# The sixth operand's low half behind the last first-layer norm, POOL's weight differences in two pieces, and one sum in halves

## The chip, the cores and the metric

The kernel runs on one core of a Trainium2 chip. The core has a matrix engine (PE, with its weight loads as PEld), a vector engine (DVE), a scalar engine (ACT), a third elementwise engine (POOL) and SyncE (SP), which issues the transfers. They run separate instruction streams and wait for one another by semaphores. The metric is device time in microseconds (us) for one execution, lower is better.

## The reference, cut to what matters

One decoder layer on 1024 tokens of width 1024, in float32. Two attentions run side by side, their outputs are gated, merged and projected, a layer norm follows, and then the MLP:

```python
merged = gate_a * (ya @ w_branch_a) + gate_b * (yb @ w_branch_b)
mix_out = merged @ w_out
x = _layer_norm(DEEPNORM_ALPHA * x + mix_out, ln1_gain, ln1_bias)   # the first-layer norm
h = square(relu(x @ w_ff1))                                        # 1024 -> 4096
ff_out = h @ w_ff2                                                 # 4096 -> 1024
x = _layer_norm(DEEPNORM_ALPHA * x + ff_out, ln2_gain, ln2_bias)
```

## The kernel before, in words

A float32 product is made of three matmuls. An operand is split into a high half (a copy rounded to the matrix engine's float32 format, made by ACT) and a low half (operand minus high half, made by DVE or POOL by one subtraction); the three matmuls are high by high, low by high and high by low.

The MLP's products use Strassen's scheme in Winograd's form: seven block products in place of eight, on sums and differences of the four blocks of each operand. In the first MLP product the seven are numbered m = 1 to 7. `x_h`, `x_l` hold the high and low halves of the activation operand of each m, `a_h`, `a_l` those of the weight operand; the work runs in eight rounds n = 0 to 7 over the 4096 hidden columns. A product (n, m) is 24 matmuls of 512 columns in two halves t = 0, 1 of 12, one PSUM bank each (`up`, L1094 to L1114). Round 0 takes m in the order 1, 2, 6, 5, 7, 4, 3 (`UP_FIRST`); the sums of the products (`take_u2`, `take_u3`, `take_c22`, ...) run on DVE. Product 7 adds to the banks of product 6, and `take_u3` adds to them `p1`, the first product, into `c22`; product 4 then adds to the same banks again, so PE may start it only when `take_u3` has read them.

The change lies where the output projection ends and round 0 begins. Tokens come in eight blocks `tb` of 128. For each, PE makes `project_out(tb)` in two halves of 24 matmuls, DVE adds the residual and norms the row block (`layer_norm1`, L1921), PE transposes the result (`turn_x1`, L1049, 8 transposes), and ACT and DVE split it (`x_high`, `x_low`) and form the sums. The last block's transposes stand inside product (0, 2), behind its ninth matmul. There is no planner: each engine's order is written by hand, and an engine that waits holds up all that stands behind it in its own order.

- DVE, after the norm of block 6 (`layer_norm1(TB - 2, 0, 64)`): `sums_low(6, 0, 3)`, the low half of the sixth activation operand for its first three column blocks (1536 columns, one subtraction with both inputs in SBUF); then the norm of block 7, between whose two halves `x_low(TB - 2)` makes low halves 1 and 2 that product (0, 1) and (0, 2) wait for; then `x_low(TB - 1)`, which reads the last transposes.
- POOL: `a_low(1)`, `a_low(2)` (low halves of weight operands, L2360), `r_s1 = r21 + r22` (L2369), `r11 = r_s1 - r11` (L2372), `a_low(6)`: five instructions of 1024 columns.
- ACT: `a_high(5, 0)`, which waits for `r_s1`, `a_high(6, 0)`, which waits for the second sum (`w_sum`), and behind it `x_high(TB - 1)`, the high halves of the last transposed block (L1414 to L1418).
- PE: product (0, 1) waits for the first low half out of `x_low(TB - 2)` (`x1_lo` 7) and for `a_lo[1]`; the transposes of block 7 wait for `x1_ready`, the end of the norm (L1918); product (0, 6) waits for `a_lo[6]` and for the sixth operand's last block (`x_low_done` 2).

In rows of the profile, L1587 is the helper that subtracts (`sub`), L1988 that of `add`, L1991 that of `minus`. Names there lack buffer numbers and last digits: `r` stands for `r11`, `r12`, `r21` and `r22`, `r_s` for `r_s1`, `b_f` for `b11_f` and `b21_f`, `t_last` for `t2_last`, `c` for `c22` and its like.

Of the kernel before, what the change touches and what calls it, by code (L numbers as in the profile page):

```python
# [18 lines left out]
F32 = mybir.dt.float32  # L19
# [70 lines left out]
for _n in range(ITERS):  # L90
    for _m in UP if _n else UP_FIRST:
        UP_END[_m, _n] = len(UP_END) + 2
# [96 lines left out]
def layer_kernel(nc, x, w_in, w_branch_a, w_branch_b, w_out, lambda_q1, lambda_k1, lambda_q2,  # L189
                 lambda_k2, subln_gain, ln1_gain, ln1_bias, w_ff1, w_ff2, ln2_gain, ln2_bias,  # L190
                 consts, rope, out):
    with ExitStack() as ctx:
# [207 lines left out]
        x22_f = sem("x22_f")  # L400
# [5 lines left out]
        up_done, p1_read, c11_read, taken = sem("up_done"), sem("p1_read"), sem("c11_read"), sem("taken")  # L406
        relu_done, h_sum = sem("relu_done"), sem("h_sum")
# [342 lines left out]
        def _(pe):  # L750
# [310 lines left out]
            def wait_up(n, m):  # L1061
# [27 lines left out]
                elif m == 4:  # L1089
                    pe.wait_ge(taken, 5 * n + 2)  # L1090
                elif m == 3:
                    pe.wait_ge(taken, 5 * n + 3)

            def up(n, m):  # L1094

                wait_up(n, m)
                for t in range(2):
                    if n == 0 and m == 2:
                        pe.wait_ge(p1_read, t + 1)
                    o = up_bank(m, t)  # L1100
# [11 lines left out]
                    if n == 0 and m == 1 and t == 0:  # L1112
# [59 lines left out]
        def _(act):  # L1172
# [229 lines left out]
            def x_high(tb):  # L1402
# [9 lines left out]
                else:  # L1412
                    act.wait_ge(t12_ready, 2 * j + 2)
                    act.activation(x_block(6, 0, j), x_sum(6, j), ACT.Copy).then_inc(t_hi, 1)  # L1414
                    act.activation(x_sum(3, j), by_block(p_proj[:, 1, :]), ACT.Copy).then_inc(x22_f, 1)
# [167 lines left out]
        def _(dve):  # L1583
# [304 lines left out]
            def layer_norm(row, tb, s, base_n, summed, scale_here, stat=None, gain=None):  # L1888
# [3 lines left out]
                for h in range(2):  # L1892
# [28 lines left out]
            def layer_norm1(tb, s, count, between=lambda: None):  # L1921
                for h in range(2):
                    if h == 1:
                        between()
# [6 lines left out]
                layer_norm(rows[s][:, :], tb, s, 0, lambda h: dve.wait_ge(o_read, tb * 2 + (h + 1)), True)\  # L1931
# [44 lines left out]
            layer_norm1(TB - 2, 0, 64)  # L1976
            sums_low(6, 0, 3)
            layer_norm1(TB - 1, 1, 64, lambda: x_low(TB - 2))
# [43 lines left out]
            def take_u3(n):  # L2022
                dve.wait_ge(up_done, UP_END[7, n])
                if n:
                    dve.wait_ge(s_h[4], 16 * n)
                    dve.wait_ge(h_sum, 4 * n - 3)
                else:
                    dve.wait_ge(s_x1[1], 64)
                    dve.wait_ge(x1_turned, 2 * TB)
                add(c22, bank_b, p1).then_inc(taken, 1)  # L2030

            def take_c22(n):
                dve.wait_ge(up_done, UP_END[5, n])
                dve.wait_ge(taken, 5 * n + 2)
                add(c22, bank_c, c22).then_inc(taken, 1)
# [215 lines left out]
        def _(pool):  # L2251
# [105 lines left out]

            def a_low(m):
                pool.wait_ge(a_hi, HIGH_END[m, 0])
                pool.tensor_tensor(al[m][:, :, :], raw[m][:, :, :], ah[m][:, :, :].bitcast(F32), ALU.subtract)\  # L2360
                    .then_inc(a_lo[m], 1)
# [39 lines left out]
```

## Time and profile before

| | |
|---|---|
| Time of three executions | 1502.28, 1504.42, 1505.61 us; median 1504.42 |
| Execution that was profiled | 1502.67 us, its span 1500.6 us |
| PE busy in the span | 1469.0 us, 98% |
| DVE, ACT, POOL busy | 990.9 us (66%), 664.2 us (44%), 353.6 us (24%) |
| Mean granted clock of PE | 0.997 of full speed |
| PE idle between 855 and 925 us | three times: 0.63, 0.77 and 1.41 us |

The span runs from the first to the last instruction; the execution's time has 2.07 us more. A matmul of 512 columns is shown with 0.39 us, but in an unbroken row the next one starts 0.227 us later, so the shown durations overlap. Idle time in brackets is that before the row, with what ended it.

### The profile page before, as it was taken

Reading aid. Unit: us, or ns where it says so; the run is one execution under the profiler, and the core shown is the slowest. Engines: PE = TensorE matmul, PEld = TensorE weight load, DVE = VectorE, ACT = ScalarE, POOL = GpSimd, SP = SyncE. Lnnn points to the kernel's source line nnn. Section 1 sums busy time; section 2 is a strip of 40 time slices with the busy share of each in tenths; the row PEclk is TensorE's granted clock in tenths of the full one; section 3 lists DMA queues with packets and bytes.
Section 4 is the critical chain, followed back from the end, with each engine's and each line's share of the span. In section 5 each row is a group of like instructions: output and inputs, shape, how many; then the busy total and the mean of one; then the engine's idle time right before and its main releaser. Section 6 shows DMA issues by size and latency. Waiting matters only on the chain.

```text
span 1500.6 us, 19376 instructions
## 1 busy us (share of the span) xinstructions
PE 1469.0 (98%) x7152; PEld 1220.7 (81%) x7152; DVE 990.9 (66%) x1232; ACT 664.2 (44%) x1035; POOL 353.6 (24%) x276
## 2 busy tenths in 40 slices
PE   8999999999999999999999999999999999999997
PEld 6788888887888887888778877888888888888886
DVE  3676776768857557444466688766664477668767
ACT  3455554556556556442022244444443434433343
POOL 2635445355444244210230040000000000000004
PEclk9999999999999999999999999999999999999999
DMA  5101112111111101011343224444442678835563
GB/s 179 57 28 57 57 43 71 56 56 54 46 57 28 29 15 42 28 57 43 126 154 127 85 98 155 182 163 149 152 154 99 237 277 277 316 123 191 193 200 135
DMA packets 111504, 172.41 MB, mean 115 GB/s; under 512 B 6080, under 2 KB 71616, under 8 KB 111296
## 3 DMA queue, kind: packets, MB, share of 16 engines
q1 hardware_dynamic: 111424, 171.33, 33.5%
q8 instruction: 51, 0.84, 0.2%
q14 instruction: 29, 0.24, 0.1%
HBM read 127.27 MB, written 44.04 MB: 114 GB/s over the span
## 4 chain that ended last, share of the span: by engine, by line
PE 87%; DVE 6%; issue 3%; DMA 2%; ACT 1%; POOL 1%; SPq 0%; DVEq 0%; ACTq 0%
PE p_proj L760 8%; PE p_proj L756 8%; PE p_proj L758 8%; PE p_z L1108 5%; PE p_z L1106 5%; PE p_z L1110 5%; PE p_z L1128 4%; PE p_z L1129 4%; PE p_z L1130 4%; PE p_tr L858 3%; PE p_z L795 2%; PE p_av L872 2%; PE p_z L791 2%; PE p_av L875 2%; PE p_proj L1108 2%
## 5 line engine op out<-in xcount | busy, mean ns | idle before, releaser
L756 PE MATMUL p_proj<-xt_h,w_hi 128*128 128x512 f32 x640 | 253.9, 397 | 0.6 <-DVE xt_l L1587 0.6
L760 PE MATMUL p_proj<-xt_h,w_lo 128*128 128x512 f32 x640 | 252.7, 395 | 0.0
L758 PE MATMUL p_proj<-xt_l,w_hi 128*128 128x512 f32 x640 | 251.2, 393 | 0.0
L2262 POOL TENSOR_TENSOR w_lo<-w_raw,w_hi 128x512 fp32r<-128x512 f32 x96 | 133.7, 1414 | 223.1 <-DVE w_hi L1594 222.6
L2378 POOL TENSOR_TENSOR row_odd<-row_odd,gains 128x1024 f32<-128x1024 f32 x4 | 10.4, 2621 | 580.1 <-ACT row_odd L1559 580.1
L760 PEld LDWEIGHTS p_proj<-xt_h,w_lo 128*128 128x128 f32 x640 | 120.3, 188 | 23.6
L756 PEld LDWEIGHTS p_proj<-xt_h,w_hi 128*128 128x128 f32 x640 | 120.4, 188 | 22.8 <-DVE xt_l L1587 0.6
L758 PEld LDWEIGHTS p_proj<-xt_l,w_hi 128*128 128x128 f32 x640 | 120.5, 188 | 20.8
L1587 DVE TENSOR_TENSOR d_al<-f_a,d_ah 128x1024 fp32r<-128x1024 f32 x56 | 68.5, 1224 | 78.8 <-ACT d_ah L1477 78.8
L1477 ACT ACTIVATE d_ah<-f_a 128x1024 fp32r<-128x1024 f32 x56 | 59.2, 1057 | 133.2 <-PE p_av L1130 54.9
L1330 ACT ACTIVATE a_t<-p_tr 128x384 fp32r<-128x384 f32 (+3 forms) x96 | 47.2, 492 | 123.6 <-PE p_tr L858 123.5
L1106 PE MATMUL p_z<-x_h,a_h 128*128 128x512 f32 x256 | 99.8, 390 | 0.6 <-DVE x_l L1587 0.6
L1110 PE MATMUL p_z<-x_h,a_l 128*128 128x512 f32 x256 | 99.6, 389 | 0.0
L1108 PE MATMUL p_z<-x_l,a_h 128*128 128x512 f32 x256 | 99.6, 389 | 0.0
L1128 PE MATMUL p_z<-d_bh,d_ah 128*128 128x512 f32 x256 | 99.6, 389 | 0.0
L1129 PE MATMUL p_z<-d_bl,d_ah 128*128 128x512 f32 x256 | 99.6, 389 | 0.0
L1130 PE MATMUL p_z<-d_bh,d_al 128*128 128x512 f32 x256 | 99.6, 389 | 0.0
L1437 ACT ACTIVATE a_h<-r 128x1024 fp32r<-128x1024 f32 x48 | 50.4, 1056 | 88.1 <-PE p_z L1110 47.6
L1587 DVE TENSOR_TENSOR a_t<-p_tr,a_t 128x384 fp32r<-128x384 f32 (+3 forms) x96 | 53.0, 552 | 52.1 <-ACT a_t L1330 51.8
L1594 DVE CAST w_hi<-w_raw 128x1024 fp32r<-128x1024 f32 x48 | 43.4, 905 | 59.5 <-DMA w_raw<-w_branch_b 34.2
L1587 DVE TENSOR_TENSOR a_l<-r,a_h 128x1024 fp32r<-128x1024 f32 x45 | 54.9, 1219 | 37.0 <-ACT a_h L1437 37.0
L1699 DVE TENSOR_REDUCE vecs<-p_z 128x1 f32<-128x128 f32 (+7 forms) x64 | 46.9, 753 | 42.0 <-PE p_z L795 41.7
(287 smaller groups left out, 3546.7 us busy)
## 6 DMA issues: line engine op xcount, KB each, us to landing
f_a<-h_terms SPq DMA_DIRECT2D x56, 512.0 KB, 3.4
w_raw<-w_in SPq DMA_DIRECT2D x40, 512.0 KB, 3.9
h_terms<-c SPq DMA_DIRECT2D x40, 512.0 KB, 3.1
f_b<-w_ff SPq DMA_DIRECT2D x40, 512.0 KB, 4.7
r<-w_ff SPq DMA_DIRECT2D x32, 512.0 KB, 4.0
gate_rows<-gst SPq DMA_DIRECT2D x12, 512.0 KB, 5.0
y<-x SPq DMA_DIRECT2D x8, 512.0 KB, 8.6
wo_raw<-w_out SPq DMA_DIRECT2D x8, 512.0 KB, 8.8
```

The source lines that it names most:

```text
L756: pe.matmul(o, w_hi[n_slot][:, k, :], xt_h[:, k, cols], start=(k == 0), stop=False)
L758: pe.matmul(o, w_hi[n_slot][:, k, :], xt_l[:, k, cols], start=False, stop=False)
L760: mm = pe.matmul(o, w_lo[n_slot][:, k, :], xt_h[:, k, cols], start=False, stop=(k == KT - 1))
L1106: pe.matmul(o, ah[m][:, k, cols], x_row(m, 0, k), start=fresh and k == 0, stop=False, skip_group_check=not fresh)
L1108: pe.matmul(o, ah[m][:, k, cols], x_row(m, 1, k), start=False, stop=False, skip_group_check=not fresh)
L1110: mm = pe.matmul(o, al[m][:, k, cols], x_row(m, 0, k), start=False, stop=k == 3, skip_group_check=not fresh)
L1128: pe.matmul(o, a_h[:, t, rws], b_h[:, t, :], start=first, stop=False, skip_group_check=more)
L1129: pe.matmul(o, a_h[:, t, rws], b_l[:, t, :], start=False, stop=False, skip_group_check=more)
L1130: return pe.matmul(o, a_l[:, t, rws], b_h[:, t, :], start=False, stop=last, skip_group_check=more)
L1477: act.activation(a_h[:, :, :], f_a[g % 2][:, :, :], ACT.Copy).then_inc(d_hi, 1)
L1587: return dve.tensor_tensor(o, a, b.bitcast(F32), ALU.subtract)
L2262: low = pool.tensor_tensor(w_lo[slot][:, ks, :], w_raw[:, ks, :], w_hi[slot][:, ks, :].bitcast(F32), ALU.subtract)
```

## The change

Four edits.

1. `sums_low(6, 0, 3)` moves on DVE from ahead of the last `layer_norm1` to behind it. In that last norm the statistics of the first half are taken ahead of `x_low(TB - 2)`, not together with those of the second half.
2. On POOL each of the five instructions becomes two of 512 columns; the semaphore is raised by the second.
3. In round 0, `take_u3` becomes two instructions, one for each half of product 7. The first raises the new semaphore `u3_half`, and the first half of product (0, 4) waits for that alone; the second half waits for `taken`. To that end product (0, 7) counts its first half in `up_done`, and the table `UP_END` shifts by one.
4. The semaphore `x22_f`, for which nothing waited, is dropped.

On DVE, around the last first-layer norm. `x_l_112` is the sixth operand's low half, `x_l_111` and `x_l_116` are those of the first and second; `rows_105` is block 7. Before:

```order
L1918 SCALAR_TENSOR_TENSOR rows_104<-rows_104,vecs,gains 128x1024 [waits dve_own]
L1587 TENSOR_TENSOR x_l_112<-x_f_120,x_h_108 128x4x384 [waits t34_ready,t_hi]
L1929 SCALAR_TENSOR_TENSOR rows_105<-rows_105,p_z 128x512 [waits row_in1,o_done]
L1587 TENSOR_TENSOR x_l_111<-p_proj,x_h_107 128x4x128 [waits x1_hi]
L1587 TENSOR_TENSOR x_l_116<-p_proj,x_h_115 128x4x128 [waits x1_hi]
L1929 SCALAR_TENSOR_TENSOR rows_105<-rows_105,p_z 128x512 [waits o_done]
L1895 BN_STATS vecs<-rows_105 128x6 [waits o_read] x2
```

The same place in the change:

```order
L1923 SCALAR_TENSOR_TENSOR rows_104<-rows_104,vecs,gains 128x1024 [waits dve_own]
L1940 SCALAR_TENSOR_TENSOR rows_105<-rows_105,p_z 128x512 [waits row_in1,o_done]
L1934 BN_STATS vecs<-rows_105 128x6 [waits o_read]
L1592 TENSOR_TENSOR x_l_111<-p_proj,x_h_107 128x4x128 [waits x1_hi]
L1592 TENSOR_TENSOR x_l_116<-p_proj,x_h_115 128x4x128 [waits x1_hi]
L1940 SCALAR_TENSOR_TENSOR rows_105<-rows_105,p_z 128x512 [waits o_done]
L1900 BN_STATS vecs<-rows_105 128x6 [waits o_read]
```

The long subtraction is gone from here, and the first half's statistics stand ahead of the two low halves that PE waits for. It comes back behind the last pass of that norm, ahead of the last transposes' first sum:

```order
L1914 TENSOR_SCALAR vecs<-vecs 128x1 [waits dve_own]
L1917 TENSOR_SCALAR vecs<-vecs 128x1 [waits dve_own]
L1923 SCALAR_TENSOR_TENSOR rows_105<-rows_105,vecs,gains 128x1024 [waits dve_own]
L1592 TENSOR_TENSOR x_l_112<-x_f_120,x_h_108 128x4x384 [waits t34_ready,t_hi]
L1956 TENSOR_TENSOR x_f_121<-p_proj,b_f 128x4x128 [waits xe_f,x1_turned]
```

What was ahead of the norm now follows it.

POOL in the same stretch, before (`a_l_130`, `a_l_131`, `a_l_132` are the low halves of weight operands 1, 2 and 6; `r_137` is `r11`):

```order
L2360 TENSOR_TENSOR a_l_130<-r_137,a_h_123 128x1024 [waits a_hi]
L2360 TENSOR_TENSOR a_l_131<-r_138,a_h_124 128x1024 [waits a_hi]
L2369 TENSOR_TENSOR r_s_141<-r_139,r_140 128x1024 [waits r22_in,r21_in]
L2372 TENSOR_TENSOR r_137<-r_s_141,r_137 128x1024 [waits a_lo1,w_sum]
L2360 TENSOR_TENSOR a_l_132<-r_137,a_h_125 128x1024 [waits a_hi]
```

And in the change:

```order
L2379 TENSOR_TENSOR a_l_130<-r_137,a_h_123 128x512 [waits a_hi]
L2379 TENSOR_TENSOR a_l_130<-r_137,a_h_123 128x512
L2379 TENSOR_TENSOR a_l_131<-r_138,a_h_124 128x512 [waits a_hi]
L2379 TENSOR_TENSOR a_l_131<-r_138,a_h_124 128x512
L2390 TENSOR_TENSOR r_s_141<-r_139,r_140 128x512 [waits r22_in,r21_in]
L2390 TENSOR_TENSOR r_s_141<-r_139,r_140 128x512
L2395 TENSOR_TENSOR r_137<-r_s_141,r_137 128x512 [waits a_lo1,w_sum]
L2395 TENSOR_TENSOR r_137<-r_s_141,r_137 128x512
L2379 TENSOR_TENSOR a_l_132<-r_137,a_h_125 128x512 [waits a_hi]
L2379 TENSOR_TENSOR a_l_132<-r_137,a_h_125 128x512
```

The order is the same, in two pieces each, and the second pieces have no wait.

DVE at the third sum of round 0 in the change (`c_147` is `c22`; before, its first two rows were one of 128x1024 at L1988, and L2038, L2040 are the halves):

```order
L2002 TENSOR_TENSOR r_138<-r_138,r_137 128x1024 [waits a_lo2,w_sum]
L2038 TENSOR_TENSOR c_147<-p_z,p_142 128x512 [waits up_done,x1_turned,s_x1_1]
L2040 TENSOR_TENSOR c_147<-p_z,p_142 128x512 [waits up_done]
L1999 TENSOR_TENSOR c_147<-p_proj,c_147 128x1024 [waits u3_half,taken,up_done]
L1592 TENSOR_TENSOR a_l_136<-r_138,a_h_129 128x1024 [waits a_hi]
L1592 TENSOR_TENSOR res_r<-res,res_r 128x16x128 [waits x1_hi,t_hi]
```

Only the split is new there; what follows keeps its order.

The diff:

```diff
--- before.py
+++ after.py
@@ -89,7 +89,7 @@
 UP_END, HIGH_END = {}, {}
 for _n in range(ITERS):
     for _m in UP if _n else UP_FIRST:
-        UP_END[_m, _n] = len(UP_END) + 2
+        UP_END[_m, _n] = len(UP_END) + (3 if _n or _m in UP_FIRST[4:] else 2)
 for _m in (1, 2, 5, 6, 7, 4, 3):
     HIGH_END[_m, 0] = len(HIGH_END) + 1
 for _n in range(ITERS):
@@ -397,13 +397,13 @@
         s_x1 = [sem("s_x1_0"), sem("s_x1_1")]
         x1_turned = sem("x1_turned")
         xe_f, x1_hi, x1_lo = sem("xe_f"), sem("x1_hi"), sem("x1_lo")
-        x22_f = sem("x22_f")
         t12_ready, t34_ready, t_hi = sem("t12_ready"), sem("t34_ready"), sem("t_hi")
         x_low_done = sem("x_low_done")
         r11_in, r12_in, r21_in, r22_in = sem("r11_in"), sem("r12_in"), sem("r21_in"), sem("r22_in")
         w_sum, a_hi = sem("w_sum"), sem("a_hi")
         a_lo = {m: sem(f"a_lo{m}") for m in UP}
         up_done, p1_read, c11_read, taken = sem("up_done"), sem("p1_read"), sem("c11_read"), sem("taken")
+        u3_half = sem("u3_half")
         relu_done, h_sum = sem("relu_done"), sem("h_sum")
         sq_done = {m: sem(f"sq_done{m}") for m in (11, 21, 12, 22)}
         s_h = {m: sem(f"s_h{m}") for m in UP}
@@ -1087,7 +1087,10 @@
                 elif m == 2 and n > 0:
                     pe.wait_ge(p1_read, n + 2)
                 elif m == 4:
-                    pe.wait_ge(taken, 5 * n + 2)
+                    if n:
+                        pe.wait_ge(taken, 5 * n + 2)
+                    else:
+                        pe.wait_ge(u3_half, 1)
                 elif m == 3:
                     pe.wait_ge(taken, 5 * n + 3)
 
@@ -1097,6 +1100,8 @@
                 for t in range(2):
                     if n == 0 and m == 2:
                         pe.wait_ge(p1_read, t + 1)
+                    if n == 0 and m == 4 and t == 1:
+                        pe.wait_ge(taken, 2)
                     o = up_bank(m, t)
                     cols = slice(t * P, (t + 1) * P)
                     fresh = m in (1, 6, 5)
@@ -1109,7 +1114,7 @@
                                   skip_group_check=not fresh)
                         mm = pe.matmul(o, al[m][:, k, cols], x_row(m, 0, k), start=False, stop=k == 3,
                                        skip_group_check=not fresh)
-                    if n == 0 and m == 1 and t == 0:
+                    if n == 0 and m in (1, 7) and t == 0:
                         mm.then_inc(up_done, 1)
                 mm.then_inc(up_done, 1)
 
@@ -1412,7 +1417,7 @@
                 else:
                     act.wait_ge(t12_ready, 2 * j + 2)
                     act.activation(x_block(6, 0, j), x_sum(6, j), ACT.Copy).then_inc(t_hi, 1)
-                    act.activation(x_sum(3, j), by_block(p_proj[:, 1, :]), ACT.Copy).then_inc(x22_f, 1)
+                    act.activation(x_sum(3, j), by_block(p_proj[:, 1, :]), ACT.Copy)
                     act.activation(x_block(3, 0, j), by_block(p_proj[:, 1, :]), ACT.Copy).then_inc(x1_hi, 1)
                     act.wait_ge(t12_ready, 2 * j + 1)
                     act.activation(x_block(5, 0, j), x_sum(5, j), ACT.Copy).then_inc(t_hi, 1)
@@ -1885,11 +1890,11 @@
             sub(m_l[0][:, last_k, :], res[:, last_k, 0:P], m_h[0][:, last_k, :]).then_inc(mt_lo, 1)
             merged_low(1, 1)
 
-            def layer_norm(row, tb, s, base_n, summed, scale_here, stat=None, gain=None):
+            def layer_norm(row, tb, s, base_n, summed, scale_here, stat=None, gain=None, halves_due=(0, 1)):
 
 
                 st = stats[s] if stat is None else stat
-                for h in range(2):
+                for h in halves_due:
                     if summed is not None:
                         summed(h)
                         own(dve.bn_stats(st[:, 6 * h:6 * h + 6], row[:, h * NH:(h + 1) * NH]))
@@ -1918,9 +1923,15 @@
                 return dve.scalar_tensor_tensor(out=row, in0=row, scalar=ln_r[s],
                                                 in1=gains[:, 1, :], op0=ALU.mult, op1=ALU.add)
 
-            def layer_norm1(tb, s, count, between=lambda: None):
+            def layer_norm1(tb, s, count, between=lambda: None, stats_early=False):
+                def summed(h):
+                    dve.wait_ge(o_read, tb * 2 + (h + 1))
+
                 for h in range(2):
                     if h == 1:
+                        if stats_early:
+                            summed(0)
+                            own(dve.bn_stats(stats[s][:, 0:6], rows[s][:, 0:NH]))
                         between()
                     dve.wait_ge(o_done, tb * 2 + (h + 1))
                     if h == 0:
@@ -1928,7 +1939,7 @@
                     cols = slice(h * NH, h * NH + NH)
                     dve.scalar_tensor_tensor(out=rows[s][:, cols], in0=rows[s][:, cols], scalar=ALPHA,
                                              in1=p_z[s][:, cols], op0=ALU.mult, op1=ALU.add).then_inc(o_read, 1)
-                layer_norm(rows[s][:, :], tb, s, 0, lambda h: dve.wait_ge(o_read, tb * 2 + (h + 1)), True)\
+                layer_norm(rows[s][:, :], tb, s, 0, summed, True, halves_due=(1,) if stats_early else (0, 1))\
                     .then_inc(x1_ready, 1)
 
             def x_low(tb):
@@ -1974,8 +1985,8 @@
                 merged_low(tb + 2, tb % 2)
                 x_low(tb)
             layer_norm1(TB - 2, 0, 64)
+            layer_norm1(TB - 1, 1, 64, lambda: x_low(TB - 2), True)
             sums_low(6, 0, 3)
-            layer_norm1(TB - 1, 1, 64, lambda: x_low(TB - 2))
             x_low(TB - 1)
 
 
@@ -2020,18 +2031,23 @@
                 add(u2, bank_b, p1).then_inc(taken, 1)
 
             def take_u3(n):
-                dve.wait_ge(up_done, UP_END[7, n])
-                if n:
-                    dve.wait_ge(s_h[4], 16 * n)
-                    dve.wait_ge(h_sum, 4 * n - 3)
-                else:
+                if n == 0:
                     dve.wait_ge(s_x1[1], 64)
                     dve.wait_ge(x1_turned, 2 * TB)
+                    dve.wait_ge(up_done, UP_END[7, 0] - 1)
+                    dve.tensor_tensor(c22[:, 0, :], up_bank(7, 0), p1[:, 0, :], ALU.add).then_inc(u3_half, 1)
+                    dve.wait_ge(up_done, UP_END[7, 0])
+                    dve.tensor_tensor(c22[:, 1, :], up_bank(7, 1), p1[:, 1, :], ALU.add).then_inc(taken, 1)
+                    return
+                dve.wait_ge(up_done, UP_END[7, n])
+                dve.wait_ge(s_h[4], 16 * n)
+                dve.wait_ge(h_sum, 4 * n - 3)
                 add(c22, bank_b, p1).then_inc(taken, 1)
 
             def take_c22(n):
                 dve.wait_ge(up_done, UP_END[5, n])
                 dve.wait_ge(taken, 5 * n + 2)
+                dve.wait_ge(u3_half, 1)
                 add(c22, bank_c, c22).then_inc(taken, 1)
 
             def take_c21(n):
@@ -2355,10 +2371,14 @@
                 pool.tensor_tensor(x_sum(7, j), x_sum(6, j), b11_f[:, :, :], ALU.subtract).then_inc(t34_ready, 1)
                 pool.tensor_tensor(x_sum(4, j), b21_f[:, :, :], x_sum(6, j), ALU.subtract).then_inc(t34_ready, 1)
 
+            pieces = (slice(0, 2), slice(2, 4))
+
             def a_low(m):
                 pool.wait_ge(a_hi, HIGH_END[m, 0])
-                pool.tensor_tensor(al[m][:, :, :], raw[m][:, :, :], ah[m][:, :, :].bitcast(F32), ALU.subtract)\
-                    .then_inc(a_lo[m], 1)
+                for ks in pieces:
+                    low = pool.tensor_tensor(al[m][:, ks, :], raw[m][:, ks, :], ah[m][:, ks, :].bitcast(F32),
+                                             ALU.subtract)
+                low.then_inc(a_lo[m], 1)
 
             for j in range(3):
                 sums(j)
@@ -2366,10 +2386,14 @@
             a_low(2)
             pool.wait_ge(r21_in, 16)
             pool.wait_ge(r22_in, 16)
-            pool.tensor_tensor(r_s1[:, :, :], r21[:, :, :], r22[:, :, :], ALU.add).then_inc(w_sum, 1)
+            for ks in pieces:
+                sums_of = pool.tensor_tensor(r_s1[:, ks, :], r21[:, ks, :], r22[:, ks, :], ALU.add)
+            sums_of.then_inc(w_sum, 1)
             pool.wait_ge(w_sum, 1)
             pool.wait_ge(a_lo[1], 1)
-            pool.tensor_tensor(r11[:, :, :], r_s1[:, :, :], r11[:, :, :], ALU.subtract).then_inc(w_sum, 1)
+            for ks in pieces:
+                sums_of = pool.tensor_tensor(r11[:, ks, :], r_s1[:, ks, :], r11[:, ks, :], ALU.subtract)
+            sums_of.then_inc(w_sum, 1)
             a_low(6)
 
             for q in range(TB - 1):
```

## Rows read from the trace of the kernel before

**Rows 1.** Timeline of PE: start us, us, engine, line, operation, shapes, count [idle before <-releaser].

```profile
878.59 0.39 PE L1031 MATMUL p_z<-wo_h,m_l 128*128 128x512 f32 x1
879.61 0.47 PE L1106 MATMUL p_z<-x_h,a_h 128*128 128x512 f32 x1 [0.63 <-DVE x_l L1587]
...
888.15 1.09 PE L1049 MATMUL p_proj<-small,rows 128*128 128x128 f32 x8 [0.77 <-DVE rows L1918]
...
892.51 0.39 PE L1106 MATMUL p_z<-x_h,a_h 128*128 128x512 f32 x1
...
908.61 0.39 PE L1110 MATMUL p_z<-x_h,a_l 128*128 128x512 f32 x1
910.41 0.47 PE L1106 MATMUL p_z<-res_r,a_h 128*128 128x512 f32 x1 [1.41 <-DVE c L1988]
...
915.93 0.39 PE L1106 MATMUL p_proj<-res_r,a_h 128*128 128x512 f32 x1
```

**Rows 2.** Timeline of DVE, 874 to 892 us.

```profile
874.33 3.94 DVE L1587 TENSOR_TENSOR x_l<-x_f,x_h 128x1536 fp32r<-128x1536 f32 x1
...
879.98 0.67 DVE L1929 SCALAR_TENSOR_TENSOR rows<-rows,p_z 128x512 f32<-128x512 f32 x1
...
882.20 2.55 DVE L1901 SCALAR_TENSOR_TENSOR rows<-rows,vecs,gains 128x1024 f32<-128x1024 f32 x1
...
885.61 2.48 DVE L1918 SCALAR_TENSOR_TENSOR rows<-rows,vecs,gains 128x1024 f32<-128x1024 f32 x1
...
891.03 0.69 DVE L1587 TENSOR_TENSOR x_l<-t_last,x_h 128x512 fp32r<-128x512 f32 x1 [0.70 <-ACT x_h L1414]
```

**Rows 3.** Timeline of POOL, 873 to 891 us.

```profile
873.38 3.27 POOL L2360 TENSOR_TENSOR a_l<-r,a_h 128x1024 fp32r<-128x1024 f32 x1 [2.50 <-ACT a_h L1437]
878.93 2.39 POOL L2360 TENSOR_TENSOR a_l<-r,a_h 128x1024 fp32r<-128x1024 f32 x1 [2.28 <-ACT a_h L1437]
881.27 2.40 POOL L2369 TENSOR_TENSOR r_s<-r,r 128x1024 f32<-128x1024 f32 x1
883.75 3.26 POOL L2372 TENSOR_TENSOR r<-r_s,r 128x1024 f32<-128x1024 f32 x1
888.24 2.40 POOL L2360 TENSOR_TENSOR a_l<-r,a_h 128x1024 fp32r<-128x1024 f32 x1 [1.23 <-ACT a_h L1437]
```

**Rows 4.** Timeline of POOL and DVE, earlier: POOL work already in two pieces.

```profile
561.31 2.98 POOL L2262 TENSOR_TENSOR w_lo<-w_raw,w_hi 128x512 fp32r<-128x512 f32 x2 [0.63 <-DVE w_hi L1594]
...
617.88 2.55 POOL L2262 TENSOR_TENSOR w_lo<-w_raw,w_hi 128x512 fp32r<-128x512 f32 x2 [13.19 <-DVE w_hi L1594]
...
562.38 0.76 DVE L1669 TENSOR_TENSOR stage<-stage,swap 128x512 f32<-128x512 f32 x1
```

**Rows 5.** Timeline of ACT, 876 to 891 us.

```profile
876.34 0.59 ACT L1411 ACTIVATE x_h<-p_proj 128x512 fp32r<-128x512 f32 x1
...
887.11 1.06 ACT L1437 ACTIVATE a_h<-r 128x1024 fp32r<-128x1024 f32 x1 [0.19 <-POOL r L2372]
890.36 0.63 ACT L1414 ACTIVATE x_h<-t_last 128x512 fp32r<-128x512 f32 x1 [2.20 <-DVE t_last L1949]
```

**Rows 6.** Timeline of DVE around the third sum of round 0.

```profile
909.03 1.23 DVE L1988 TENSOR_TENSOR c<-p_z,p 128x1024 f32<-128x1024 f32 x1 [1.85 <-PE p_z L1110]
910.36 1.23 DVE L1988 TENSOR_TENSOR c<-p_proj,c 128x1024 f32<-128x1024 f32 x1
...
912.64 2.29 DVE L1587 TENSOR_TENSOR res_r<-res,res_r 128x2048 fp32r<-128x2048 f32 x1
```

**Rows 7.** Stretches: from:to, length, busy of PE, PEld, DVE, ACT, POOL, granted clock, DMA.

```profile
671.00:675.00 4.00, 4.00 (x11) 3.13 (x10) 0.00 (x0) 2.62 (x3) 0.00 (x0) 0.50 0.01 2
782.50:785.30 2.80, 0.00 (x0) 0.03 (x1) 2.80 (x3) 0.00 (x0) 0.48 (x1) 1.00 0.00 0
...
1492.50:1493.00 0.50, 0.28 (x2) 0.00 (x0) 0.18 (x1) 0.00 (x0) 0.49 (x1) 1.00 0.00 0
...
1497.50:1498.00 0.50, 0.00 (x0) 0.00 (x0) 0.50 (x1) 0.00 (x0) 0.00 (x0) 0.75 0.02 8
```

## The prediction

> **What bounds the kernel now.** I read the shares of the page first: PE is busy for 98% of the span, so only its few gaps can be won or lost. The timeline of PE over the stretch that the change touches shows three of them, which a DVE instruction ends each time: 0.63 us ahead of product (0, 1), 0.77 ahead of the last transposes, 1.41 ahead of product (0, 4) [rows 1]. In an unbroken row a matmul starts 0.227 us after the last and is shown with 0.39, so a gap costs its idle time plus 0.16: 879.61 - 878.59 - 0.23 = 0.79, then 0.93, then 910.41 - 908.61 - 0.23 = 1.57 [rows 1]. A product of 24 matmuls takes 5.44 us, but 5.52 behind a gap (910.41 to 915.93) [rows 1]: 0.08 to 0.12 more for each. All that the change can win is thus 3.29 + 0.3 = some 3.6 us, 0.24% of the time; 0.2%, 3.0 us, is about what a measurement of this kernel can tell from no change.
>
> Then I read DVE and POOL side by side, and that is the view that decides here. The 1536-column subtraction takes 3.94 us, and 2048 columns take 2.29 elsewhere [rows 2, 6]. POOL was at work until 873.38 + 3.27 = 876.65, and DVE ends 1.62 us after that. The norm's two passes show the same: POOL ends at 883.67 and DVE's pass at 884.75, 1.08 later; POOL at 887.01, DVE at 888.09, 1.08 later [rows 2, 3]. And the other way round: POOL's second sum starts at 883.75 behind that DVE pass and takes 3.26 in place of 2.40 [rows 3]. So a DVE instruction that reads two tensors from SBUF and a POOL instruction shut each other out, and the later one waits for the end of the earlier. With one input from PSUM DVE is free of it (879.98: 0.67 us while POOL is at work) [rows 2, 3].
>
> **The change part by part.** I run the clock of before on from 874.33, where DVE's order first differs.
>
> *The move.* Without the subtraction DVE does the first half row at 874.33 and its statistics, and is idle when ACT ends the first high half at 876.34 + 0.59 = 876.93 [rows 5]. The low half that PE waits for is there at 877.6, not 879.5; PE comes at 878.59 + 0.23 = 878.82 and goes on. Gap 1 is gone: 0.79 + 0.12. DVE takes the second half row 0.42 us after PE's last matmul's start (the lag of 908.61 to 909.03) [rows 1, 6], at 879.01 in place of 879.98. From there to the norm's first pass it took 2.22 us [rows 2]; one set of statistics less (0.60) makes 1.62, so that pass is ready at 880.63.
>
> *The pieces.* Two pieces take 2.55 us where one instruction takes 2.39 [rows 3, 4], so 0.15 more for each of the five. What happens between the pieces is seen in the earlier stretch: two pieces from 561.31 take 2.98, and a DVE pass issued at 562.38 ends at 563.14, that is 0.56 us after the first piece (561.31 + 1.27); the second ends 1.15 after DVE [rows 4]. DVE slips in between and POOL pays. With these numbers, in turn: POOL's second low half 878.93 to 881.47; DVE's first pass to 882.55; POOL piece to 883.70; DVE's second pass, ready at 883.4 (its small steps take 885.61 - 884.75 = 0.86 [rows 2]), to 884.78. The row block is normed at 884.8 in place of 888.09. PE reaches the transposes at 878.82 + 33 x 0.227 = 886.3: gap 2 is gone too, 0.93 + 0.1.
>
> The Trainium skill ("SBUF — State Buffer", section "Who interferes with whom") says of this port pair that issue order, not the shape of the operation, decides who blocks. By it the DVE pass that was issued first goes ahead of POOL's second piece; [rows 4] agree, with 0.56 us behind the first piece. Were it otherwise, rival B below would hold.
>
> *What the move now lands on.* Behind the norm stands the 1536-column subtraction. It is ready at 884.8, in the middle of POOL's sums, where before it had delayed only DVE. POOL's piece goes to 885.93, the subtraction to 887.55 (1.62), POOL's second sum to 888.70 and, unhindered, 889.97 (before: 887.01). Three DVE instructions, 1.08 + 1.08 + 1.62 = 3.78 us, now lie inside POOL's chain of second low half and two sums, where one pass of 1.08 lay before. For this sum ACT waits with the high half of weight operand 6: 890.07 to 891.13 (before 887.11) [rows 5], and POOL's low half of it starts at 891.20, not 888.24 [rows 3]. ACT's next, the high half of the last block, starts at 891.0 in place of 890.36 and gives DVE its low half (two SBUF inputs) at 891.7; that slips between POOL's pieces: 892.46, DVE to 893.01, POOL to 894.16. Before, POOL was done at 890.64 and PE came at 892.51, so 1.9 us of cover lay there [rows 1, 3]. Now PE comes at 886.3 + (892.51 - 888.15) = 890.67 and may go on about 0.15 us after 894.16 (DVE's 909.03 + 1.23 let PE go at 910.41 [rows 1, 6]), at 894.3. A new gap: 3.6 us, as idle time 3.5, in front of product (0, 6), which starts 1.8 us later than before. For the bounds of this unknown: with neither the subtraction nor the low half in POOL's way (2.17 us less) it starts at 892.1; with one more DVE pass in the way (1.1 to 2.2) at 895.4 to 896.5.
>
> *The third sum.* Product (0, 4)'s first half needs only the first half of the sum, which DVE can make while PE does product 7's second half (DVE was idle for 1.85 us there [rows 6]). Gap 3 goes: 1.57 + 0.08. Product (0, 4) starts at 894.3 + 5.52 + 2 x 5.44 = 910.70 (before 910.41). DVE is 0.54 us sooner with its sums, since 0.69 stands where 1.23 was; but the low half for product (0, 3) ended at 912.64 + 2.29 = 914.93 and PE came at 915.93 [rows 1, 6], with 1.0 us of cover less lag. In the new clock it is there at 916.25 and lets PE go at 916.40, while PE comes at 916.14: a small gap, 0.26 + 0.08.
>
> *Sum.* Won: 0.91 + 1.03 + 1.65 = 3.6. Lost: 3.6 + 0.1 + 0.34 = 4.05. Product (0, 3) ends 0.5 us later than before. From there to the end PE has no gap in either, so the shift goes through. The dropped semaphore, the extra one in `take_c22` and 8 instructions more on POOL and DVE, off PE's path, cost nothing: `u3_half` is raised before the sum that asks for it. The profiled execution took 1502.67 us and becomes 1503.2; the median of the runs shown is 1.75 above it, so the forecast is 1504.9.
>
> **The rivals.** *A. The port's delays fall elsewhere and the new gap stays away*: 3.6 - 0.34 = 3.25 us won, 1501.2. For it: a DVE pass in POOL's way costs nothing where POOL has time, as before at 1.9 us of cover. Against it: POOL's chain would have to be 3.6 us shorter than I find, nearly all of the 4.3 us of DVE work that I put into it, and PE comes 1.85 us sooner.
>
> *B. POOL keeps the port through both pieces.* Then DVE's first pass waits for the end of POOL's first sum (884.0, to 885.1), the second for that of the second sum (887.5, to 888.6); the transposes start 0.55 later than before, product (0, 6) too, and gap 3 less 0.34 is won: 0.55 - 1.65 + 0.34 = -0.75, 1503.7. Against it: DVE's pass between two pieces at 562.38 [rows 4].
>
> *C. The new gap lets PE's clock fall*, and the kernel is slower. The longest gap in the middle of the program is 2.8 us and the clock stayed at 1.00; after the last matmul (ended 1492.78) it was still 1.00 at first and 0.75 in the half microsecond from 1497.5, so it fell within 4.7 to 5.2 us [rows 7]. My gap of 3.5 lies between. If it falls, matmuls run as at 671 to 675, at 0.50, the lower level of 1.2 GHz: 11 in 4 us [rows 7] where 4 / 0.227 = 17.6 fit, so 4 us of it lose 1.5, and 6 us at half the pace lose 3. The time is then 0.5 + 1.5 to 3 above: 1506.4 to 1507.9, about 1507.2. It decides between 2.8 and 4.7 us of idle time in front of product (0, 6); a gap of 4.5, if one more DVE pass comes in between, brings it near.
>
> **How the numbers follow.** Forecast 75%, A 6%, B 7%, C 12%. The forecast's own range is what the bounds give: product (0, 6) 2.2 sooner to 2.2 later, of which I hold the ends unlikely, so -1.5 to +2 with the spread of the runs (1502.28 to 1505.61) around the median: 1502.4 to 1506.9. C lies at the upper edge, A below the lower: I take 1502.0 to 1507.2. Slower by over 0.2% (above 1507.4) is half of C and a bad tail, 9%; faster by over 0.2% (under 1501.4) is A and a little, 7%; within 84%.
>
> **What would show it.** In the profile after: no gap in front of product (0, 1) nor of the last transposes; POOL's pieces of the two sums with three waits of 1.1 to 1.6 us among them, ending near 890; ACT's high half of operand 6 starting about 3 us later than 887.11; a gap of 3 to 4 us in front of product (0, 6), ended by POOL's low half; none in front of product (0, 4), one of some 0.1 to 0.3 in front of (0, 3). The forecast is wrong if POOL's last low half ends under 891, if DVE's passes wait through both pieces, or if the granted clock is under 1.00 after that gap.

## The result, and the profile after

The changed kernel takes 1507.74 us in the median of 21 executions, the one before 1504.65 us in 21 of its own: a ratio of 1.0020, 95% interval 1.0013 to 1.0028, so 2.0 to 4.2 us slower. The forecast was 0.5 us slower and the range ended at 1507.2. The profiled execution took 1506.52 us, span 1504.7.

The timeline of PE in the changed kernel, where before had its three gaps (columns as in [rows 1]; L1111 is the old L1106, L2379 the old L2360, L1999 the old L1988); the last row is from round 1:

```profile
891.92 0.39 PE L1115 MATMUL p_z<-x_h,a_l 128*128 128x512 f32 x1
895.71 0.80 PE L1111 MATMUL p_z<-x_h,a_h 128*128 128x512 f32 x1 [3.40 <-POOL a_l L2379]
896.30 0.63 PE L1113 MATMUL p_z<-x_l,a_h 128*128 128x512 f32 x1
896.73 0.63 PE L1115 MATMUL p_z<-x_h,a_l 128*128 128x512 f32 x1
...
902.85 0.39 PE L1111 MATMUL p_proj<-x_h,a_h 128*128 128x512 f32 x1
...
918.95 0.39 PE L1115 MATMUL p_z<-res_r,a_l 128*128 128x512 f32 x1
919.37 0.47 PE L1111 MATMUL p_proj<-res_r,a_h 128*128 128x512 f32 x1
...
952.68 0.47 PE L1111 MATMUL p_z<-res_r,a_h 128*128 128x512 f32 x1 [0.38 <-DVE c L1999]
```

All three gaps of [rows 1] are gone. In their place stand one of 3.40 us in front of product (0, 6), ended by POOL's low half, one of 0.19 in front of product (0, 3) (919.37 - 918.95 - 0.23; the rows show no idle time for it), and one of 0.38 in round 1. And behind the first of them matmuls are shown with 0.63 us and start 0.43 apart, not 0.23: product (0, 6) takes 902.85 - 895.71 = 7.14 us where 5.52 was its time. The stretches show why (columns as in [rows 7]):

```profile
785.00:786.00 1.00, 0.78 (x4) 0.67 (x5) 1.00 (x2) 0.00 (x0) 0.00 (x0) 1.00 0.00 0
...
787.00:788.00 1.00, 1.00 (x4) 0.81 (x3) 0.62 (x2) 0.45 (x2) 0.00 (x0) 0.50 0.00 0
...
894.00:895.00 1.00, 0.00 (x0) 0.00 (x0) 1.00 (x2) 0.65 (x2) 1.00 (x1) 1.00 0.00 0
895.00:896.00 1.00, 0.29 (x1) 0.29 (x2) 1.00 (x1) 0.00 (x0) 0.66 (x1) 0.85 0.00 0
896.00:897.00 1.00, 1.00 (x3) 0.81 (x3) 1.00 (x3) 0.76 (x2) 0.00 (x0) 0.50 0.00 0
897.00:898.00 1.00, 1.00 (x3) 0.72 (x3) 1.00 (x1) 0.47 (x1) 0.00 (x0) 0.50 0.00 0
```

The granted clock fell to 0.50 (1.2 GHz) at the end of the new gap, and 8 matmuls ran at it: 8 x 0.2 = 1.6 us. It also fell near 786 us, 1.2 us after the end of the 2.82 us gap that both kernels have. In the profile of before it had stayed at 1.00 in that gap [rows 7] and behind it:

```profile
785.30:790.00 4.70, 4.70 (x21) 3.88 (x22) 3.63 (x4) 1.26 (x2) 0.00 (x0) 1.00 0.27 77
```

Timelines of DVE, POOL and ACT in the changed kernel, for the chain that ends the new gap:

```profile
875.85 0.68 DVE L1940 SCALAR_TENSOR_TENSOR rows<-rows,p_z 128x512 f32<-128x512 f32 x1
...
882.32 1.76 DVE L1906 SCALAR_TENSOR_TENSOR rows<-rows,vecs,gains 128x1024 f32<-128x1024 f32 x1
...
884.93 1.38 DVE L1923 SCALAR_TENSOR_TENSOR rows<-rows,vecs,gains 128x1024 f32<-128x1024 f32 x1
886.24 2.84 DVE L1592 TENSOR_TENSOR x_l<-x_f,x_h 128x1536 fp32r<-128x1536 f32 x1
```

```profile
880.46 2.54 POOL L2379 TENSOR_TENSOR a_l<-r,a_h 128x512 fp32r<-128x512 f32 x2 [2.13 <-ACT a_h L1442]
882.95 4.52 POOL L2390 TENSOR_TENSOR r_s<-r,r 128x512 f32<-128x512 f32 x2
887.54 3.95 POOL L2395 TENSOR_TENSOR r<-r_s,r 128x512 f32<-128x512 f32 x2
892.72 2.94 POOL L2379 TENSOR_TENSOR a_l<-r,a_h 128x512 fp32r<-128x512 f32 x2 [1.23 <-ACT a_h L1442]
```

```profile
891.58 1.06 ACT L1442 ACTIVATE a_h<-r 128x1024 fp32r<-128x1024 f32 x1 [2.96 <-POOL r L2395]
```

DVE reaches its first changed instruction at 875.85 here, not 874.33: this execution is 1.52 us later before the change begins. The fall near 786 us accounts for that: PE had started its output projection 0.08 us sooner (785.22 for 785.30) and then had 8 slow matmuls. Less 1.52, DVE's two passes end at 882.56 and 884.79, the moved subtraction at 887.56, POOL's second sum at 889.97, ACT starts at 890.06, and POOL ends at 894.14. The forecast had 882.55, 884.78, 887.55, 889.97, 890.07, 894.16.

### The profile page after: what moved, and what is told of

It is laid out like the page before. It is cut to its first block and busy times, and to the rows that moved or that the text cites. A ratio compares the mean times of both kernels' runs of the same rounds, so it can differ in the third digit from the quotient of the medians.

```text
span 1504.7 us, 19382 instructions
## 1 busy us (share of the span) xinstructions
PE 1471.7 (98%) x7152; PEld 1223.2 (81%) x7152; DVE 989.8 (66%) x1233; ACT 664.3 (44%) x1035; POOL 356.5 (24%) x281
## 5 line engine op out<-in xcount | busy, mean ns | idle before, releaser
L756 PE MATMUL p_proj<-xt_h,w_hi 128*128 128x512 f32 x640 | 253.8, 397 | 0.6 <-DVE xt_l L1592 0.6
L756 PEld LDWEIGHTS p_proj<-xt_h,w_hi 128*128 128x128 f32 x640 | 120.4, 188 | 22.7 <-DVE xt_l L1592 0.6
L1111 PE MATMUL p_z<-x_h,a_h 128*128 128x512 f32 x256 | 100.6, 393 | 3.4 <-POOL a_l L2379 3.4
L1115 PE MATMUL p_z<-x_h,a_l 128*128 128x512 f32 x256 | 100.1, 391 | 0.0
```

Source lines behind the costliest of these rows:

```text
L756: pe.matmul(o, w_hi[n_slot][:, k, :], xt_h[:, k, cols], start=(k == 0), stop=False)
L1111: pe.matmul(o, ah[m][:, k, cols], x_row(m, 0, k), start=fresh and k == 0, stop=False, skip_group_check=not fresh)
L1115: mm = pe.matmul(o, al[m][:, k, cols], x_row(m, 0, k), start=False, stop=k == 3, skip_group_check=not fresh)
```

## The experiments

In the profiles of all these kernels the first matmul of the output projection (L1029; L1031 where a filling stands ahead of it) starts anywhere from 783.7 to 788.1 us, far ahead of the change. So beside the medians I compare, for each profile, the time from that matmul to the end of the span, and the same with 0.2 us taken off for each matmul at the low clock behind it ("without the clock"). That is one profile for each kernel, and those of the changed kernel with and without fillings lie between 716.3 and 716.8: differences of 0.5 us there tell nothing. The medians are of 9 to 12 executions (21 for the first two rows), and each ratio is to executions of the kernel before taken at the same time, whose median was 1504.65 for the second row, 1504.77 for the next four, 1504.45 for the four behind them and 1504.14 for the last four.

| Kernel | median, us | ratio to before (95%) | from first L1029 to end | slow matmuls | without the clock |
|---|---|---|---|---|---|
| before | 1504.65 | 1 | 1500.6 - 785.30 = 715.3 | 0 | 715.3 |
| changed | 1507.74 | 1.0020 (1.0013 to 1.0028) | 1504.7 - 785.22 = 719.5 | 8 + 8 | 716.3 |
| after_again | 1507.80 | 1.0020 (1.0011 to 1.0029) | 1508.6 - 787.45 = 721.2 | 9 + 13 | 716.8 |
| filled_gap | 1505.95 | 1.0012 (1.0001 to 1.0023) | 1503.3 - 787.01 = 716.3 | 0 | 716.3 |
| no_move | 1505.71 | 1.0007 (0.9997 to 1.0016) | 1503.9 - 787.20 = 716.7 | 0 + 8 | 715.1 |
| no_pieces | 1503.46 | 0.9989 (0.9980 to 0.9999) | 1500.4 - 783.69 = 716.7 | 8 + 0 | 715.1 |
| halves_only | 1504.48 | 1.0000 (0.9991 to 1.0008) | 1502.9 - 786.34 = 716.6 | 8 + 0 | 715.0 |
| low6_on_dve | 1507.55 | 1.0016 (1.0004 to 1.0028) | 1506.7 - 788.09 = 718.6 | 8 + 8 | 715.4 |
| second_sum_on_dve | 1501.58 | 0.9982 (0.9971 to 0.9994) | 1499.8 - 786.43 = 713.4 | 8 + 0 | 711.8 |
| both_filled | 1500.31 | 0.9975 (0.9965 to 0.9984) | 1497.2 - 784.92 = 712.3 | 0 | 712.3 |
| before_early | 1504.68 | 1.0004 (0.9991 to 1.0017) | 1502.3 - 787.04 = 715.3 | 0 | 715.3 |
| after_early | 1506.90 | 1.0018 (1.0009 to 1.0027) | 1505.4 - 786.37 = 719.0 | 0 + 13 | 716.4 |
| after_both | 1504.88 | 1.0006 (0.9994 to 1.0017) | 1502.1 - 785.82 = 716.3 | 0 | 716.3 |
| halves_early | 1503.36 | 0.9997 (0.9986 to 1.0008) | 1503.0 - 787.37 = 715.6 | 0 | 715.6 |

Slow matmuls are those behind the gap near 782 + those behind the one in front of product (0, 6).

### The changed kernel again

> The changed kernel once more, as the base for the three beside it. Theory: POOL's chain of low half and two sums is some 3 us late in it, PE stands idle for 3.4 us in front of product (0, 6), its granted clock falls behind that gap nearly every time (1.5 us), and DVE owes 0.6 us in round 1: 0.5 + 1.5 + 0.6 = 2.6 us above the kernel before. Rival: the fall of the clock in the one profile was chance, and then most executions are only 1.1 us above.

Measured: 1507.80 us, the same as in the first 21 executions, and its profile has a gap of 3.39 us and the low clock again, for longer (columns as in [rows 7]):

```profile
896.00:897.00 1.00, 0.00 (x0) 0.00 (x0) 1.00 (x2) 0.85 (x2) 1.00 (x2) 0.96 0.00 0
897.00:898.00 1.00, 0.09 (x1) 0.09 (x1) 1.00 (x1) 0.00 (x0) 0.86 (x1) 0.50 0.00 0
...
899.00:903.00 4.00, 4.00 (x11) 3.13 (x10) 4.00 (x4) 0.67 (x2) 0.00 (x0) 0.50 0.00 0
```

13 slow matmuls cost 2.6 us here. The median is 3.0 us above before, 2.6 expected; the gap in round 1 is 0.89 us here, 0.38 in the first profile. The other executions were not profiled, but each has its mean granted clock: the mean over them is 0.9939 in the first 21 and 0.9942 in these 10, against 0.9958 to 0.9962 in the three sets of 33 to 35 of the kernel before. A fall of 8 slow matmuls takes 8 x 0.43 x 0.5 / 1505 = 0.0011 off it, so the changed kernel has between one and two such falls more on average. The fall was no chance.

### The gap filled with matmuls

> The changed kernel with 8 matmuls of 512 columns (1.8 us) ahead of product (0, 6), into its own banks, which product (0, 6) then overwrites. They use up idle time of PE and delay nothing. If the clock is what costs: no stretch under 1.00 behind the gap, product (0, 6) in 5.5 us and not 7.1, and 1.5 us less than the changed kernel. If only the waiting costs and the clock does not: the same time as the changed kernel within 0.3 us.

```diff
+                if n == 0 and m == 6:
+                    pe.wait_ge(o_read, 2 * TB)
+                    for i in range(8):
+                        pe.matmul(up_bank(6, i % 2), xh[1][:, 0, 0:P], x_row(1, 0, 0), start=True, stop=True)
                 wait_up(n, m)
```

Measured: 1505.95 us, 1.85 under the same kernel without them (1.5 expected). Timeline of PE and the stretch behind it (the added lines shift the numbers: L1115 is L1111 of the changed kernel, L2383 its L2379):

```profile
892.29 1.98 PE L1102 MATMUL p_z<-x_h 128*128 128x512 f32 x8
895.88 0.50 PE L1115 MATMUL p_z<-x_h,a_h 128*128 128x512 f32 x1 [1.61 <-POOL a_l L2383]
896.21 0.40 PE L1117 MATMUL p_z<-x_l,a_h 128*128 128x512 f32 x1
...
901.45 0.39 PE L1115 MATMUL p_proj<-x_h,a_h 128*128 128x512 f32 x1
```

```profile
896.00:900.00 4.00, 4.00 (x18) 3.31 (x19) 4.00 (x4) 1.23 (x2) 0.00 (x0) 1.00 0.00 0
```

Product (0, 6) still waits for the same POOL instruction and starts no sooner; only the idle time ahead of it is 1.61 us, the clock stays at 1.00, and the product takes 5.57 us (901.45 - 895.88), not 7.14. The mean granted clock of the 12 executions is 0.9957, about that of before. More work on PE made the kernel faster: the clock was the cost. The intervals of the two ratios overlap in part; the pair of after_early and after_both below shows the same difference once more.

### The move undone, the pieces undone

> The changed kernel with the sixth operand's low half back ahead of the last norm (and the statistics together again); pieces and halves stay. Theory (move and pieces do harm together, since three DVE instructions then lie inside POOL's chain): gaps 1 and 2 stay away all the same, as the subtraction waits for half a POOL instruction only; POOL's low half of operand 6 ends 1.6 us sooner, the gap in front of product (0, 6) is 1.9 to 2.1 us; 2.1 us less than the changed kernel without the clock, 0.5 under the kernel before, if the clock holds. Rival (the pieces alone are the loss): still 2 us or more above before.

```diff
-            layer_norm1(TB - 1, 1, 64, lambda: x_low(TB - 2), True)
             sums_low(6, 0, 3)
+            layer_norm1(TB - 1, 1, 64, lambda: x_low(TB - 2))
```

> The changed kernel with POOL's five instructions whole again; move and halves stay. Theory: POOL's second sum then goes ahead of the moved subtraction, its low half of operand 6 ends near 892.0 on the clock of before, and the gap in front of product (0, 6) is about 2 us: 0.5 under the kernel before if the clock holds. Rival (the move alone is the loss): the gap stays at 3.4 us and the time at that of the changed kernel.

```diff
-            pieces = (slice(0, 2), slice(2, 4))
+            pieces = (slice(0, 4),)
```

The gaps in the timeline of PE, of no_move first, then of no_pieces:

```profile
894.70 0.79 PE L1111 MATMUL p_z<-x_h,a_h 128*128 128x512 f32 x1 [2.01 <-POOL a_l L2379]
951.87 0.47 PE L1111 MATMUL p_z<-res_r,a_h 128*128 128x512 f32 x1 [0.56 <-DVE c L1999]
```

```profile
892.52 0.47 PE L1111 MATMUL p_z<-x_h,a_h 128*128 128x512 f32 x1 [1.75 <-DVE x_l L1592]
948.28 0.47 PE L1111 MATMUL p_z<-res_r,a_h 128*128 128x512 f32 x1 [0.77 <-DVE c L1999]
```

The gaps at the change are as worked out: no gap 1 or 2 in either, 2.01 and 1.75 us in front of product (0, 6) in place of 3.40. Those of 0.56 and 0.77 in round 1 were not worked out. Each edit alone was enough against gaps 1 and 2; together they put three DVE instructions into POOL's chain. Without the clock both stand at 715.1, 1.2 under the changed kernel and 0.2 under before. Their medians (1505.71 and 1503.46) are 2.25 us apart. In the profiles the clock fell behind the gap of 2.01 us and not behind that of 1.75, and over all executions the mean granted clock is 0.9947 and 0.9963: the clock is then worth some 1.6 of the 2.25. The profiles themselves do not show the difference, since in that of no_pieces the clock fell behind the early gap instead (716.7 in both). For no_move I had forecast 0.5 under before and got 0.9 above; the gap came as worked out, and I had wrongly held the clock for safe at 2 us. For no_pieces the forecast was 0.5 under too, and the median is 1.3 under.

### The halves alone

> The kernel before with the third sum in halves and nothing else of the change. Theory: gaps 1 and 2 stay as they were (0.63 and 0.77 us), gap 3 goes (1.65 won), a gap of 0.3 to 0.4 comes in front of product (0, 3) and DVE, which was saved only 0.54 us, gives 0.6 back in round 1: 0.7 us under the kernel before. Rival (all that PE wins there stays): 1.65 under.

The edit is the third sum's alone. Measured: no change, 1504.48 us. Its profile has gaps 1 and 2 as before (0.64, 0.81), none in front of product (0, 4), 0.19 in front of (0, 3) (its first matmul starts at 917.13, the one before it at 916.71), and one in round 1, here in the timelines of PE and DVE:

```profile
950.76 0.47 PE L1111 MATMUL p_z<-res_r,a_h 128*128 128x512 f32 x1 [0.70 <-DVE c L1999]
```

```profile
937.59 1.23 DVE L1999 TENSOR_TENSOR r_s<-r,r 128x1024 f32<-128x1024 f32 x1 [0.59 <-DMA r<-w_ff]
```

In the kernel before DVE goes without a break from 934.19 to 949 us; here it waits 0.59 us for the load of the next weights, and the third sum of round 1, which PE then needs, comes late. The gain of 1.65 is more than half a loan: 0.2 to 0.3 go back in front of product (0, 3) and 0.85 in round 1. The rival, 1.65 under, is out: the ratio's interval ends at 1.4 under.

### The low half of operand 6 on DVE

> The changed kernel with the low half of weight operand 6 made by DVE (1.2 us) and not by POOL (2.9 us in two pieces), ahead of the last block's low half. Theory: the end of POOL's second sum sets the gap, so that it shrinks by the difference alone, to some 2.3 us idle: 1.3 us less than the changed kernel, 2.8 if the clock then holds.

```diff
+            a_low(6, 0)
             sums_low(6, 3, 4)
```

and `a_low(6)` deleted on POOL. The gap is 2.33 us as expected (ended by DVE's low half of the last block), and without the clock the kernel is 0.9 to 1.4 us under the changed one. But the clock fell behind this gap too, 1.2 us after PE had started again, and the median (1507.55) shows nothing of a gain, where 1.3 us had been expected.

### The second sum on DVE

> A version meant to beat both: order of DVE as before, POOL in pieces, the third sum in halves; the second weight sum and the low half of operand 6 go from POOL to DVE, into its idle time ahead of the last transposes and while it waits for ACT; the low half for product (0, 3) stands between the halves of the third sum. Theory: no gap on PE from 870 to 960 us, no fall of the clock there, 3.5 us under the kernel before. If I have the port wrong, a gap stays in front of product (0, 6).

```diff
# DVE, ahead of x_low(TB - 1); deleted on POOL with a_low(6)
+            dve.wait_ge(w_sum, 1)
+            dve.wait_ge(a_lo[1], 1)
+            dve.tensor_tensor(r11[:, :, :], r_s1[:, :, :], r11[:, :, :], ALU.subtract).then_inc(w_sum, 1)
             x_low(TB - 1)
...
+            a_low(6, 0)
             sums_low(6, 3, 4)
...
# in take_u3, between the halves; deleted behind a_low(3, 0)
+                    sums_low(3, 0, 4)
```

with the move undone. Measured: 1501.58 us, ratio to before 0.9982 (0.9971 to 0.9994). Timeline of DVE:

```profile
888.72 1.22 DVE L1992 TENSOR_TENSOR r<-r_s,r 128x1024 f32<-128x1024 f32 x1 [1.18 <-POOL r_s L2394]
889.86 0.68 DVE L1956 TENSOR_TENSOR x_f<-p_proj,b_f 128x512 f32<-128x512 f32 x1
890.64 0.69 DVE L1960 TENSOR_TENSOR t_last<-p_proj,x_f 128x512 f32<-128x512 f32 x1
891.25 1.22 DVE L1592 TENSOR_TENSOR a_l<-r,a_h 128x1024 fp32r<-128x1024 f32 x1
```

DVE makes in 2.4 us what took POOL 5.7 in the kernel before (3.26 + 2.40 [rows 3]) and 6.9 in the changed one, largely in its own idle time, and from 800 to 1200 us the profile shows no wait of PE at all. Without the clock the profile is 3.5 us under before, the 3.5 forecast; the median is 2.9 under, with the clock down behind the early gap in the profile.

### The early gap filled

> The same, with 8 matmuls of 512 columns ahead of the first output projection, in the 2.8 us gap near 782 us that both kernels have; their result is read by nothing. If the clock falls behind that gap in a part of the executions (as in the changed kernel's profile, not in that of before), this saves 1.5 us in those: up to 1 us in the median. If it hardly ever falls there: the same time as the version without.

```diff
                 if first:
+                    for i in range(8):
+                        pe.matmul(p_tr[:, :], y_h[:, 0, 0:P], y_h[:, 0, 0:NH], start=True, stop=True)
                     pe.wait_ge(mt_first_lo, 1)
```

Measured: 1500.31 us (1498.76 to 1500.82), ratio 0.9975 (0.9965 to 0.9984): 4.1 us under the 1504.45 of before at that time, and the fastest of all. The narrow spread led me to a second theory, that the clock behind the early gap makes most of the spread of every version, and to four kernels with that filling:

> The kernel before with 8 matmuls of 512 columns in the 2.8 us gap near 782 us, read by nothing. Theory: the clock falls behind that gap in a part of the executions and that is most of the spread of 6 to 7 us between them; with it filled the spread shrinks to about 2 us, and the median lies 1 us or so under the kernel before. Rival: the spread has another source (transfers), and neither changes.

> The changed kernel with the same filling near 782 us only, so that the gap in front of product (0, 6) stays. Against before_early: 0.5 from the gaps, 0.6 to 0.9 from DVE's debt in round 1, 1.5 from the clock behind the new gap, together 2.6 to 2.9 us. Rival (the fall there is an exception): 1.1 to 1.4 us.

> The changed kernel with both gaps filled. Theory: 1.5 us under after_early, and 1.1 to 1.4 us above before_early: what the change costs without the clock. If the clock plays no part: the same as after_early.

> The third sum in halves alone, with the filling near 782 us. Alone it came out at no change, within 1.3 us. Its profile shows 1.41 us of idle time gone and 0.70 back in round 1: with the quieter base that is 0.7 to 0.8 us under before_early. Rival (all is given back later): the same as before_early within 0.3.

The second theory fell: before_early spreads from 1500.06 to 1509.01 us and its median is that of before. Much of the spread comes from ahead of 785 us, as the starts of the first matmul of the output projection show, and the traces say where. Up to 3 us are there at the first L811 (662.5 to 665.5 us), most of it from the start: the first L756 starts anywhere from 13.4 to 16.6 us, and why is open. Up to 3.2 us more are the clock again, near 670 us, where it is low in every profile but not for the same time; some 1 us comes between there and the output projection. Stretches of no_pieces, of before and of low6_on_dve:

```profile
670.00:672.00 2.00, 2.00 (x8) 1.57 (x7) 0.00 (x0) 1.95 (x3) 0.00 (x0) 0.66 0.02 4
674.00:676.00 2.00, 2.00 (x14) 1.82 (x14) 0.56 (x3) 0.23 (x1) 0.00 (x0) 1.00 0.00 0
```

```profile
670.00:672.00 2.00, 2.00 (x9) 1.81 (x8) 0.00 (x0) 0.80 (x2) 0.00 (x0) 0.50 0.02 7
674.00:676.00 2.00, 2.00 (x11) 1.62 (x9) 0.00 (x0) 0.00 (x0) 0.00 (x0) 0.71 0.00 0
```

```profile
670.00:672.00 2.00, 2.00 (x11) 2.00 (x11) 0.00 (x0) 0.00 (x0) 0.00 (x0) 0.50 0.37 112
674.00:676.00 2.00, 2.00 (x6) 1.56 (x6) 0.00 (x0) 1.75 (x3) 0.00 (x0) 0.50 0.02 4
```

The same work of PE, from the first L811 to the first L997, takes 16.1 us in the first of them, 17.7 in the second and 19.3 in the third. The shortest time is that of no_pieces and both_filled, the longest that of low6_on_dve and no_move, and the ten others have 17.7. So the profile of both_filled was lucky by 1.6 us there, its narrow spread may be luck too, and what its filling alone gives is open (1.3 us between the medians, in intervals that overlap). The first theory held: after_early is 2.2 us above before_early (2.6 to 2.9 expected, 1.1 to 1.4 if the fall were an exception), after_both 2.0 under after_early (1.5) and 0.2 above before_early by the medians, 1.0 by the profiles (1.1 to 1.4). halves_early is 1.3 under before_early by the medians (0.7 to 0.8 expected), which hardly tell it from nothing, and 0.3 above in the profile, where the gap in round 1 has 1.47 us. That gap is 0.27 to 1.47 us long in ten of the twelve profiles with the halves, and in each of the ten DVE waits for the load (0.20 to 0.85 us); low6_on_dve has no such wait and no idle time there (its matmul starts 0.22 late), second_sum_on_dve a wait of 0.26 and no gap. What sets its length is open.

## Why the prediction was wrong

The end: 3.1 us slower, forecast 0.5. Step by step:

- *The move, gaps 1 and 2.* Right; both are gone.
- *The pieces; what the move lands on.* Right to 0.02 us at six points of the chain, and the new gap has 3.40 us idle against 3.5. Rival B (POOL goes through both its pieces ahead of DVE) and A are out. That each of the two edits alone leaves about 2 us of gap was worked out the same way and measured (2.01 and 1.75).
- *The third sum.* Gap 3 went; the small gap in front of product (0, 3) was 0.19 against 0.26.
- *"From there to the end PE has no gap in either."* Wrong by 0.6 us in the first profile (0.38 idle, 0.16, and 0.08 for the start), by 1.1 in the second. I followed DVE only to the end of round 0. In round 1 its third sum had a cover of about 0.1 us, since PE went on at 948.58 without a gap and DVE's sum had ended at 948.35; and in the changed kernel DVE waits 0.27 us for a load there, which it does not in the kernel before.
- *Rival C, the clock.* The step that failed, and most of the miss: the sum of the forecast has no term for the clock, at a new gap of 3.5 us, and the fall had a chance of 12%. I took one gap of 2.8 us with the clock at 1.00 for a lower bound, and put the point of decision between 2.8 and 4.7 us. Neither bound holds. In nine profiles with that gap the clock fell behind it in six. It fell in three of three behind 3.4 us, behind 2.33 and 2.01 us, and not behind 1.75, 1.61 and 1.61. And after the last matmul of the program, where my 4.7 to 5.2 us came from, the same fall came after anything from 2.2 us (second_sum_on_dve) to 5.0 (before). One row at full clock had told me only of one execution, and that of [rows 7] ends with the gap, where a fall can come later. The price, 1.5 to 3 us, was right: 1.6 and 2.6.

The sum that the profiles show: 0.5 for the gaps, 0.6 in round 1, 1.6 to 2.6 for the clock behind the new gap: 2.7 to 3.7, in the interval of 2.0 to 4.2. Where the clock is held up by fillings (after_both against before_early), the profiles are 1.0 us apart, the 0.5 + 0.6 of this sum; the medians are 0.2 apart.

## What to carry to other kernels

Where two edits relieve the same wait, work out each alone: here each freed PE, and together they delayed the engine that feeds it next. A gap that comes into an otherwise unbroken row of matmuls has to be priced with the clock from about 2 us on (the shortest with a fall here was 2.01 us), and whether the clock falls must be read from several executions; matmuls with no use, in place of idle time, are a cheap test and sometimes a remedy. Follow a gain through the next round of the engine that it comes to depend on.

## What the runs showed of the hardware

- The granted clock may fall after PE has started again: at 786.46, 1.2 us behind a gap of 2.82 us that ended at 785.22, and 1.2 us behind one of 2.33 us. It may also fall inside the gap (after_again, about 1 us before its end).
- At one and the same place of the program the low clock lasts for different times from execution to execution: 8 or 13 slow matmuls behind the new gap, and 16.1, 17.7 or 19.3 us for the same work near 670 us.
- POOL and DVE instructions that both read two tensors from SBUF take turns at each instruction's end even where both have more work waiting. The six POOL pieces of the second low half and the two sums took 11.0 us (880.46 to 891.49) with three DVE instructions among them, where three pairs take 3 x 2.55 = 7.65 [rows 4]: 3.4 us more.
- The same program up to its first output projection reaches it between 783.7 and 788.1 us.
